# The out-products of the second block and its mixing product computed as three fp32r passes in all their rows

## What is computed

```
h  = h + 0.5*gt1*swiglu(ada_norm(h, ...), w1_ffn1, w3_ffn1, w2_ffn1)
u  = ada_norm(h, g_mix, sh2, sc2)
g0, g1, g2 = split(sigmoid(u @ w_bgate + b_bgate), 3)
h  = h + gt2 * ((g0*y_conv + g1*y_mla + g2*y_four) @ w_out)
h  = h + 0.5*gt3*swiglu(ada_norm(h, ...), w1_ffn2, w3_ffn2, w2_ffn2)
swiglu(x, w1, w3, w2) = (silu(x @ w1) * (x @ w3)) @ w2        # 1024 -> 2816 -> 1024
```

## Time and profile before

| | |
|---|---|
| median of 3 timed executions | 3303.55 us (3299.9 to 3307.59) |
| profiled execution, its time | 3296.33 us |
| its span, first to last instruction | 3294.2 us |
| mean granted TensorE clock, share of full | 0.966 |
| busy TensorE, VectorE, ScalarE, GpSimd | 94%, 42%, 32%, 2% |
| ffn1_out, layer 1, from its first to its last float32 record | 1282.46 to 1422.8 us |
| ffn2_out, last layer, likewise | 3210.49 to 3282.1 us |
| mix_out, first and last layer | 56.91 us, 27.90 us |

### The profile page before, as it was taken

The page is one execution under the profiler, slowest core; times in us unless marked ns, Lnnn a source line. Parts: engine busy times, 40 slices in busy tenths (PEclk is TensorE's granted clock), DMA queues, the critical chain, the costliest instruction groups (busy, mean ns, idle before and its releaser), DMA issues.

```text
span 3294.2 us, 44271 instructions
## 1 busy us (share of the span) xinstructions
PE 3109.2 (94%) x16514; PEld 2395.2 (73%) x16514; DVE 1369.8 (42%) x2363; ACT 1058.2 (32%) x1664; POOL 69.6 (2%) x46
## 2 busy tenths in 40 slices
PE   6998999998988999999899989999999998899998
PEld 6856998856987886566466648875588756678897
DVE  5344656334654222249234242231322215654442
ACT  4333644333633222023355212220222203365341
POOL 0000000000000000012000000000000001100000
PEclk9899999899998999999999999999999998999999
DMA  4576554576543232221221212222222222234454
GB/s 166 161 262 217 167 177 143 165 254 226 166 154 130 98 99 85 83 78 39 67 72 58 77 64 96 96 88 83 74 99 96 86 81 88 82 95 137 148 180 132
DMA packets 119870, 400.74 MB, mean 122 GB/s; under 512 B 13008, under 2 KB 22608, under 8 KB 119504
## 3 DMA queue, kind: packets, MB, share of 16 engines
q1 hardware_dynamic: 116816, 393.27, 36.7%
q10 hardware_dynamic: 2944, 6.00, 0.5%
HBM read 398.17 MB, written 1.05 MB: 121 GB/s over the span
## 4 chain that ended last, share of the span: by engine, by line
PE 84%; DVE 9%; DVEq 2%; DMA 2%; ACT 2%; issue 2%; ACTq 0%; SPq 0%
PE bank L732 18%; PE bank L739 17%; PE bank L742 17%; PE bank L1314 10%; PE bank L1976 4%; DVE hid L2220 3%; PE bank L2112 3%; PE bank L814 2%; PE bank L1339 2%; PE bank L1369 1%; DMA ring<-weights 1%; DVEq L2223 1%; DVE work L1835 1%; PE bank L2056 1%; DVE hn_lo L880 1%
## 5 line engine op out<-in xcount | busy, mean ns | idle before, releaser
L742 PE MATMUL bank<-hn_lo,w_hi 128*128 128x256 f32 (+1 forms) x3232 | 1037.5, 339 | 0.2
L739 PE MATMUL bank<-hn_hi,w_hi 128*128 128x256 f32 (+1 forms) x3232 | 1037.1, 339 | 0.0
L692 ACT ACTIVATE w_hi<-ring 128x1024 fp32r<-128x1024 f32 x468 | 495.7, 1059 | 1491.0 <-PE bank L732 979.5
L703 DVE TENSOR_TENSOR w_lo<-ring,w_hi 128x1024 fp32r<-128x1024 f32 x448 | 548.8, 1225 | 908.3 <-ACT w_hi L692 906.9
L732 PE MATMUL bank<-hn_hi,w_lo 128*128 128x256 f32 (+1 forms) x3232 | 690.5, 355 | 59.1 <-ACT hn_hi L865 20.8
L742 PEld LDWEIGHTS bank<-hn_lo,w_hi 128*128 128x128 f32 x3232 | 624.3, 193 | 67.3 <-DVE hn_lo L880 4.4
L739 PEld LDWEIGHTS bank<-hn_hi,w_hi 128*128 128x128 f32 x3232 | 625.1, 193 | 62.8
L732 PEld LDWEIGHTS bank<-hn_hi,w_lo 128*128 128x128 f32 x3232 | 525.4, 193 | 189.4 <-issue 99.7
L1314 PE MATMUL bank<-hid,ring 128*128 128x512 f32 (+1 forms) x896 | 343.0, 539 | 4.5 <-DVE hid L1916 4.5
L1314 PEld LDWEIGHTS bank<-hid,ring 128*128 128x128 f32 x896 | 169.1, 190 | 161.0 <-issue 153.8
L1916 DVE TENSOR_TENSOR hid<-bank,work 128x512 f32 (+3 forms) x88 | 55.0, 625 | 238.2 <-PE bank L742 238.2
(11 more groups left out here) (275 smaller groups left out, 2410.4 us busy)
## 6 DMA issues: line engine op xcount, KB each, us to landing
ring<-weights SPq DMA_DIRECT2D x692, 512.0 KB, 3.4
ring<-weights SPq DMA_DIRECT2D x32, 384.0 KB, 3.1
ring<-weights SPq DMA_DIRECT2D x32, 256.0 KB, 2.6
ring<-weights SPq DMA_DIRECT2D x32, 192.0 KB, 2.4
con<-consts ACTq DMA_DIRECT2D x1, 2048.0 KB, 14.1
ring<-weights SPq DMA_DIRECT2D x16, 128.0 KB, 2.0
con<-consts ACTq DMA_DIRECT2D x1, 1088.0 KB, 6.2
res<-x_cm ACTq DMA_DIRECT2D x1, 1024.0 KB, 10.3
```

The source lines that it names most:

```text
L692: act.activation(w_hi[:, even, 0:w], ring[:, slot, 0:w], ACT.Copy).then_inc(s.w_hi, 1)
L703: eng.tensor_tensor(w_lo[:, even, 0:w], ring[:, slot, 0:w], w_hi[:, even, 0:w].bitcast(F32), ALU.subtract).then_inc(s.w_lo, 1)
L739: pe.matmul(dst, high, x_hi(k), start=False, stop=False)
L742: mm = pe.matmul(dst, high, x_lo(k), start=False, stop=(stop and k == order[-1]))
```

## The change

All three chunks of ffn1_out and ffn2_out are split, and mix_out's chunk too. The activations are split where they are made: ffn_dve writes its product to tmp3, copies it as hid_hi and subtracts to hid_lo; the last branch does the same with mrg. hid_lo and mrg_lo lie in the work buffer, hid_hi in hid's place, and the sum of squares uses another scratch tile. The copies to hn_hi and hn_lo between the stages are gone. The first chunk of the following product is now split in the last group of the one before, as in the other split products.

```diff
-        order += [("ffn1", l, FF2, (8, 8), (0, 1)), ("ffn1_out", l, 8, (8, 8, 6), (1,)),
+        order += [("ffn1", l, FF2, (8, 8), (0, 1)), ("ffn1_out", l, 8, (8, 8, 6), (0, 1, 2)),
...
-                  ("mix_out", l, 8, (8,), ()), ("ffn2", l, FF2, (8, 8), (0, 1)),
-                  ("ffn2_out", l, 8, (8, 8, 6), (1,))]
+                  ("mix_out", l, 8, (8,), (0,)), ("ffn2", l, FF2, (8, 8), (0, 1)),
+                  ("ffn2_out", l, 8, (8, 8, 6), (0, 1, 2))]
...
+        hid_hi = nc.alloc_sbuf_tensor_at("hid_hi", [P, FF2, 2 * T], F32R, offset=hid_at)
+        hid_lo_a = nc.alloc_sbuf_tensor_at("hid_lo_a", [P, FF2 - 2, 2 * T], F32R, offset=work_at + 4 * 4096)
+        hid_lo_b = nc.alloc_sbuf_tensor_at("hid_lo_b", [P, 2, 2 * T], F32R, offset=work_at + 4 * 2048)
+        mrg_hi = nc.alloc_sbuf_tensor_at("mrg_hi", [P, KT, 2 * T], F32R, offset=hid_at + 4 * 10 * 2 * T)
+        mrg_lo = nc.alloc_sbuf_tensor_at("mrg_lo", [P, KT, 2 * T], F32R, offset=work_at + 4 * 4096)
...
+        def hidden_product(pe, lin, g, before, w):
+
             for c in range(lin.cpg):
...
-                for k in range(lin.tiles[c]):
-                    mm = pe.matmul(bank[2 * parity(lin, g)][:, 0:w], ring[:, slot_of(lin, g, c), k * P:(k + 1) * P],
-                                   x(row), start=(row == 0), stop=(row == last))
...
+                row = 8 * c
+                split_product(pe, lin, g, c, bank[2 * parity(lin, g)][:, 0:w],
+                              lambda part, k: pe.wait_ge(s.hid_lo, before + row + k + 1),
+                              lambda k: hid_hi[:, row + k, 0:w], lambda k: hid_low(row + k)[:, 0:w],
+                              start=(c == 0), stop=(c == lin.cpg - 1))
...
-            dve.tensor_tensor(sq[:, 0, c0:c1], res[:, k, c0:c1], res[:, k, c0:c1], ALU.mult)
+            dve.tensor_tensor(pr_b[:, c0:c1], res[:, k, c0:c1], res[:, k, c0:c1], ALU.mult)
...
-            for k in range(KT):
-                act.activation(hn_hi[:, k, 0:norm_width(n)], hid2[:, KT + k, 0:norm_width(n)],
-                               ACT.Copy).then_inc(s.hid_hi, 1)
...
-                splits_ahead(split_low, dve, lin, g)
+                splits_ahead(split_low, dve, lin, g, out)
...
-                dve.tensor_tensor(hid2[:, g.m, 0:w], bank[2 * q + 1][:, 0:w], tmp2[:, q, 0:w],
+                dve.tensor_tensor(tmp3[:, q, 0:w], bank[2 * q + 1][:, 0:w], tmp2[:, q, 0:w],
                                   ALU.mult).then_inc(drained[q], 1)
+                dve.drain()
+                dve.tensor_copy(hid_hi[:, g.m, 0:w], tmp3[:, q, 0:w])
+                dve.drain()
+                low = hid_low(g.m) if isinstance(g.m, int) else hid_lo_a[:, g.m, :]
+                dve.tensor_tensor(low[:, 0:w], tmp3[:, q, 0:w], hid_hi[:, g.m, 0:w].bitcast(F32),
+                                  ALU.subtract).then_inc(s.hid_lo, 1)
...
+            if b == 2:
+                dve.drain()
+                dve.tensor_copy(mrg_hi[:, g.m, 0:w], mrg[:, g.m, 0:w])
+                dve.drain()
+                dve.tensor_tensor(mrg_lo[:, g.m, 0:w], mrg[:, g.m, 0:w], mrg_hi[:, g.m, 0:w].bitcast(F32),
+                                  ALU.subtract).then_inc(s.mrg_lo, 1)
...
-                for k in range(KT):
-                    mm = pe.matmul(bank[2 * parity(lin, g)][:, 0:w], ring[:, slot_of(lin, g, 0), k * P:(k + 1) * P],
-                                   mrg[:, k, 0:w], start=(k == 0), stop=(k == KT - 1))
...
+                split_product(pe, lin, g, 0, bank[2 * parity(lin, g)][:, 0:w],
+                              lambda part, k: pe.wait_ge(s.mrg_lo, KT * l + k + 1),
+                              lambda k: mrg_hi[:, k, 0:w], lambda k: mrg_lo[:, k, 0:w])
...
-            first_split(split_high, act, PLAN["ffn2", l])
+            for g in turns(act, PLAN["mix_out", l], tail=2):
+                splits_ahead(split_high, act, PLAN["mix_out", l], g, PLAN["ffn2", l])
```

More of the change, by code:

```diff
@@ L484, in __init__ @@
         self.norm_hi = sem("norm_hi")
-        self.hid_hi = sem("hid_hi")
         self.hid_lo = sem("hid_lo")
@@ L490, in __init__ @@
         self.mix_lo = sem("mix_lo")
+        self.mrg_lo = sem("mrg_lo")
         self.up_v = sem("up_v")
@@ L532, in kernel_program @@
         small = sb("small", [P, 404])
-        hid2 = hid[:, :].rearrange("p (m t) -> p m t", t=2 * T)
         sq = work[:, 4096:8192].rearrange("p (m t) -> p m t", t=2 * T)
@@ L1296, in dense_t, with hid_low @@
                 input_product(pe, lin, g, 0, bank[2 * parity(lin, g)][:, 0:w], norm, w)
[L1298 to L1304, removed]
+        def hid_low(row):
+            return hid_lo_a[:, row, :] if row < FF2 - 2 else hid_lo_b[:, row - FF2 + 2, :]
+        def hidden_product(pe, lin, g, before, w):
             for c in range(lin.cpg):
[L1306 to L1312, removed]
-                for k in range(lin.tiles[c]):
-                    mm = pe.matmul(bank[2 * parity(lin, g)][:, 0:w], ring[:, slot_of(lin, g, c), k * P:(k + 1) * P],
-                                   x(row), start=(row == 0), stop=(row == last))
-                    row += 1
-                mm.then_inc(used[slot_of(lin, g, c)], 1)
+                row = 8 * c
[3 more added lines that the diff above has]
+                              start=(c == 0), stop=(c == lin.cpg - 1))
         def block1_pe(pe, l):
@@ L1542, in square @@
         def square(dve, k, c0, c1):
-            dve.tensor_tensor(sq[:, 0, c0:c1], res[:, k, c0:c1], res[:, k, c0:c1], ALU.mult)
+            dve.tensor_tensor(pr_b[:, c0:c1], res[:, k, c0:c1], res[:, k, c0:c1], ALU.mult)
             dve.drain()
-            return dve.tensor_tensor(sumsq[:, c0:c1], sumsq[:, c0:c1], sq[:, 0, c0:c1], ALU.add)
+            return dve.tensor_tensor(sumsq[:, c0:c1], sumsq[:, c0:c1], pr_b[:, c0:c1], ALU.add)
         def add_to_residual(dve, lin, following, context=False, layer=None):
@@ L1868, in ffn_pe @@
                 wait_banks(pe, lin, g)
-                hidden_product(pe, lin, g, lambda k: hid2[:, k, 0:w], w)
+                hidden_product(pe, lin, g, FF2 * (2 * l + which // 2), w)
         def gated_pair(pe, lin, n, w):
@@ L1883, in ffn_act @@
             for g in turns(act, lin, tail=2):
-                splits_ahead(split_high, act, lin, g)
+                splits_ahead(split_high, act, lin, g, PLAN["ffn1_out" if which == 0 else "ffn2_out", l])
                 act.wait_ge(used[slot_of(lin, g, 0)], turn_of(lin, g, 0) + 1)
@@ L1915, in ffn_dve @@
                 q = parity(lin, g)
-                dve.tensor_tensor(hid2[:, g.m, 0:w], bank[2 * q + 1][:, 0:w], tmp2[:, q, 0:w],
+                dve.tensor_tensor(tmp3[:, q, 0:w], bank[2 * q + 1][:, 0:w], tmp2[:, q, 0:w],
                                   ALU.mult).then_inc(drained[q], 1)
-            if out.split:
-                first_split(split_low, dve, out)
-                for k in range(KT):
-                    dve.wait_ge(s.hid_hi, KT * hid_split_number(out) + k + 1)
-                    dve.tensor_tensor(hn_lo[:, k, 0:w], hid2[:, KT + k, 0:w], hn_hi[:, k, 0:w].bitcast(F32),
-                                      ALU.subtract).then_inc(s.hid_lo, 1)
+                dve.drain()
[4 more added lines that the diff above has]
+                                  ALU.subtract).then_inc(s.hid_lo, 1)
             n = 2 * DEPTH + 3 * l + which
@@ L1981, in after_branch @@
         def after_branch(l, b):
-            return PLAN[BRANCHES[b + 1][0], l] if b < 2 else None
+            return PLAN[BRANCHES[b + 1][0] if b < 2 else "mix_out", l]
         def branch_act(act, l, b, g):
@@ L2109, in block2_pe @@
                 wait_banks(pe, lin, g)
-                wait_weights(pe, lin, g, 0)
-                for k in range(KT):
-                    mm = pe.matmul(bank[2 * parity(lin, g)][:, 0:w], ring[:, slot_of(lin, g, 0), k * P:(k + 1) * P],
-                                   mrg[:, k, 0:w], start=(k == 0), stop=(k == KT - 1))
-                mm.then_inc(used[slot_of(lin, g, 0)], 1)
+                split_product(pe, lin, g, 0, bank[2 * parity(lin, g)][:, 0:w],
+                              lambda part, k: pe.wait_ge(s.mrg_lo, KT * l + k + 1),
+                              lambda k: mrg_hi[:, k, 0:w], lambda k: mrg_lo[:, k, 0:w])
             ffn_pe(pe, l, 2)
```

## The result

The changed kernel takes 3226.49 us (median of 4 executions, 3220.0 to 3231.63) against 3305.57 us before (4 executions, 3299.9 to 3311.79). The ratio is 0.9773 with a 95% interval of 0.9748 to 0.9798. The medians are 79.1 us apart, the profiled executions, 3220.00 and 3296.33 us, 76.3; the forecast was 74.6 us less and 3229 us.

A forecast was written before the change was run, and what follows sets the result against it. TensorE was taken to bound the changed stages. Terms of 61.0 + 3.5 + 11.4 + 2.9 - 4.2 gave 74.6 us less, from the median of 3303.55 to 3229 us, range 3213 to 3245.

The forecast's parts named there:

- three 512-column out-products: ffn1_out of both layers and ffn2_out of the first: 2.54 us less per group, times 24, 61.0 us less.
- mix_out of the first layer: Mixing product of the first layer: eight split products take 43.5 us instead of 54.95, 11.4 us less.
- 2.7 us against 4.08 and 5.44: 512-column out-products: weights are split after about 2.7 us, products last 4.08 (six tiles) or 5.44 us, so nothing waits.
- That rival: Passes alone count: float32 time shrinks by a quarter in the changed products, 94.5 us less, 3209 us; chance 0.04.
- ffn2's added work: Last layer's ffn2: copy and subtraction per group delay the next low part, 0.2 us in 21 groups, 4.2 us more.
- six-tile product's wait: Last layer's ffn2_out: 2.16 us product, split 2.7; wait and restart 0.64 us in seven groups, 4.5 us given back.
- last mixing product: Last layer's mix_out, 256 columns: 4.9 us less, 2.0 given back for waits behind the residual, 2.9 us less.
- 3.5 + 2.9 - 4.2: Last layer's terms: ffn2_out 3.5 us less, mixing product 2.9 us less, ffn2's added copy and subtraction 4.2 us more.
- the one in which the 256-column waits do not arise: Rival: splits are always in time at 256 columns too, 85.3 us less, 3218 us; chance 0.12.
- that in which they are twice as large: Rival: VectorE becomes the bound at 256 columns, given-back terms double, saving 63.9 us, time 3240; chance 0.15.
- The slower one: Rival: newly split out-products and mix_out each wait out a 2.7 us split, 141 us slower, 3445; chance 0.02.

The follow-up runs named there:

- doubled copy: The changed kernel with the copy to hid_hi made twice in every group of the ffn products; 3232.49 us in one execution.
- two-pass kernel: The changed kernel with the out-products leaving out the pass w_lo times x_hi, low parts still made and waited for; 3103.40 us in one execution.
- e1_mix_float: The changed kernel with mix_out back in float32; 3240.32 us, ratio 0.982 to the kernel before.

## Why the prediction was right

The three 512-column out-products were forecast to take 61.0 us less and took 61.1 less, mix_out of the first layer 11.4 and 11.5. The step that carried them was to price a new product by the distance between two starts of the same kind of product in another stage, and not by the recorded length of a matmul. That nothing waits there at 512 columns was argued from 2.7 us against 4.08 and 5.44; the doubled copy and the two-pass kernel show it, the latter also where it ends: at 3.63 us per product a third of a microsecond per group comes back.

The Trainium skill (FP8 and Floating Point Precision, TensorE Precision Notes) gives true FP32 four passes; three in place of four would, as an estimate from that, leave 75% of the float32 time. The trace disagrees with the estimate at both widths: 5.44 / 8 over 0.859 is 79%, 2.88 / 8 over 0.432 is 83%. That rival is out.

In the last layer the sum was near, with terms off in both directions:

- *ffn2's added work* was charged 0.2 us per group and cost 0.28, 5.4 us over the stage for 4.2. A part of the miss is rounding: the row of down gave 0.24, which is 5.0 us in 21 groups. The rest is that the low part starts 1.71 us after TensorE's first matmul at one boundary, as forecast, and 1.88 at the next. At the first the 1.70 came out by luck too: VectorE started 0.31 us after TensorE and not 0.42, while the copy and the subtraction wait 0.19 and 0.15 us for "issue", where I had allowed 0.15 for all gaps. Both write to places that the loop computes, and that this is the gap is likely: the same pair in the last branch waits 0.17 to 0.19 and 0.15 us in the groups inside the loop and 0.09 and 0.07 in the two behind it, where the places are fixed. No run tried it.
- *The six-tile product's wait* was charged 0.64 us per group and cost 8.61 - 7.92 = 0.69. The mechanism and its size hold; the split takes 2.76 us from start to start, not 2.7.
- *The last mixing product* gained 2.8 us for 2.9, but not by the working given. A product takes 2.94 us and not the 3.18 of the forecast (2.88 and 0.3): I had taken the length of a single boundary of down for a steady state. Here VectorE starts on the residual 0.20 us after the product's first matmul, where down has 0.32, and on the low part 1.62 us after it and not 1.74. Instead the first product took 4.51 us, most of it at the lower clock, 1.6 us that were in no term. Two errors cancelled, which is luck.

Taken together the last layer gained 0.5 us of its 279.3. The forecast had it at 2.2 (3.5 + 2.9 - 4.2): right in sign, a quarter of the size. Of the rivals, the one in which the 256-column waits do not arise falls by the chain, and that in which they are twice as large falls too. The slower one, in which a split doesn't run beside the product before it, falls too: in the two-pass kernel products of 1.92 us start 2.85 apart, which is the split alone, and not the two one behind the other.

The absolute forecast of 3229 us was 2.5 above the median. The range of 32 us was wider than the terms needed, since the 512-column ones had rows that fixed them.

## What to carry over

Price a changed instruction by the distance between starts in a stage that runs it already, and its preparation by the time from the start of one product to the readiness of the next; the change pays in full where the shortest product is longer than that preparation, whatever the average share of the preparing engine. Here the same edit won 20 us in a stage of 512 columns and next to nothing at 256. Before it is given up there, look at what is queued behind the added step: the subtraction, moved behind the next step in line, cost nothing, and then the change paid at 256 columns as well.

## What was not expected of the hardware

The matmuls of type fp32r start 0.2267 us apart at 512 columns and 0.1200 at 256. Per column that is 0.417 ns, one column per cycle of 2.4 GHz, and at both widths 13.3 ns are left over per matmul. Float32 records start 0.4291 and 0.2158 us apart, 0.833 ns or two cycles per column, which leaves some 2.5 ns over. So the price of three fp32r matmuls against a float32 tile depends on the width only through this fixed part and is not the ratio of passes. What the 13 ns are, the weight load of each matmul or something else, stays open; VectorE and ScalarE do not cause it, since the distance is the same whether they work or stand still within a product.

And the clock. Ahead of the last mixing product TensorE stands still for 1.91 us in the two kernels where it is float32 (before, and `e1_mix_float`), and the granted clock stays full through it. In the ten profiles in which it is split, the pause is 2.02 to 2.05 us, and in every one of them the clock falls to the lower level 0.4 to 1.2 us after the product's start, for about 3.4 us. That costs the 1.6 us above. It is not the stages ahead that matter: in `e1_mix_float` they are as changed, but for what prepares mix_out's split itself. Nor is it the length of the pause alone: in the first profile of the change a pause of 2.03 us, 42 us before this one, left the clock at full. Which difference decides it, the 0.1 us more of pause, its place in time or the work behind it, no run here tells. In the first layer's mixing product the pause is longer, 2.66 us before and 2.79 after, and the clock falls for 3.4 us both times; that is most of the 1.96 us of its start, of which the change won next to nothing (1.9 us after it).
